# VectorE multiplies and sums two cached key pages in one operation, and eight more pages stand in the projections

## What is computed

```python
past_k = cache_k[l][page_table].reshape(n_seq, n_pages * PAGE_SIZE, B_HEADS, B_HEAD_DIM)
...
s_past = (jnp.einsum('bqhd,bkhd->bhqk', q, past_k).astype(jnp.float32) * scale
          + F_new[..., None] - F_past)
...
p = jax.nn.softmax(jnp.concatenate([s_past, s_new], axis=-1), axis=-1)
```

## Time and profile before

| | |
|---|---|
| median of 3 runs | 2400.07 us |
| lowest and highest | 2394.64, 2401.17 us |
| the profiled execution: time, span | 2381.5 us, 2379.8 us |
| TensorE busy in the span | 1949.2 us (82%) |
| VectorE busy | 1640.2 us (69%) |
| GpSimd busy | 1291.0 us (54%) |

### The profile page before, as it was taken

The page is one execution under the profiler, slowest core; times in us unless marked ns, Lnnn a source line. Parts: engine busy times, 40 slices in busy tenths (PEclk is TensorE's granted clock), DMA queues, the critical chain, the costliest instruction groups (busy, mean ns, idle before and its releaser), DMA issues.

```text
span 2379.8 us, 30517 instructions
## 1 busy us (share of the span) xinstructions
PE 1949.2 (82%) x10334; PEld 815.0 (34%) x10334; DVE 1640.2 (69%) x3898; ACT 313.1 (13%) x675; POOL 1291.0 (54%) x1562
## 2 busy tenths in 40 slices
PE   5999999897889978878886788996776766776677
PEld 4444444534556775323331133331111111111111
DVE  2898899665544388666667876577787786767642
ACT  1112233521121121110000101010000000000000
POOL 1343333144443245666667766666666666666674
PEclk8999999999999989999999999999999999999899
DMA  9786787797787569999999999999999999999997
GB/s 332 263 271 210 247 280 247 232 350 240 257 278 244 185 225 383 404 389 404 402 387 378 392 404 404 402 389 390 377 370 368 378 358 382 363 369 366 376 381 282
DMA packets 264649, 794.62 MB, mean 334 GB/s; under 512 B 33328, under 2 KB 64788, under 8 KB 263992
## 3 DMA queue, kind: packets, MB, share of 16 engines
q0 software_dynamic: 191008, 680.63, 76.9%
q1 hardware_dynamic: 73504, 112.20, 13.7%
HBM read 781.60 MB, written 11.11 MB: 333 GB/s over the span
## 4 chain that ended last, share of the span: by engine, by line
PE 28%; POOL 27%; DVE 16%; issue 13%; DMA 9%; another core or an unknown queue 6%; ACT 1%; SPq 0%; PEld 0%; POOLq 0%; DVEq 0%; PEldq 0%; ACTq 0%
POOL arena L1022 27%; PE banks L1047 11%; DVE arena L2981 5%; PE banks L1349 3%; DMA arena<-in_peer_v,arena 2%; PE banks L1480 2%; DMA arena<-in_cache_v 2%; DMA arena<-in_peer_u,arena 2%; PE banks L1684 2%; DMA arena<-in_w_ada 2%; DVE arena L2196 1%; PE banks L1225 1%; PE banks L1232 1%; DVE arena L2201 1%
## 5 line engine op out<-in xcount | busy, mean ns | idle before, releaser
L1684 PE MATMUL banks<-arena 128*32 128x512 f32 x2048 | 906.9, 625 | 302.7 <-DMA arena<-in_peer_v,arena 204.1
L2981 DVE CUSTOM_DVE_ANT_0 arena<-arena,banks 128x1024 f32<-128x1024 f32 x496 | 601.8, 1216 | 261.6 <-DMA arena<-in_peer_u,arena 187.3
L1022 POOL DMA_INDIRECT arena<-in_peer_v,arena x520 | 501.4, 964 | 305.1 <-issue 157.7
L1022 POOL DMA_INDIRECT arena<-in_peer_u,arena x520 | 504.8, 971 | 220.9 <-issue 152.6
L1684 PEld LDWEIGHTS banks<-arena 128*32 128x32 f32 x2048 | 178.1, 112 | 948.2 <-issue 528.3
L1047 PE MATMUL banks<-arena 128*128 128x128 f32 (+6 forms) x1352 | 352.0, 417 | 8.9 <-DVE arena L2259 2.7
L1753 ACT ACTIVATE arena<-banks 128x512 f32<-128x512 f32 (+12 forms) x360 | 154.5, 429 | 1163.1 <-remote 263.2
L998 POOL DMA_DIRECT2D arena<-in_cache_k x256 | 137.8, 538 | 282.5 <-DVE arena L2201 184.8
L1047 PEld LDWEIGHTS banks<-arena 128*128 128x128 f32 (+1 forms) x1352 | 216.6, 195 | 146.0 <-issue 129.2
L998 POOL DMA_DIRECT2D arena<-in_cache_v x256 | 138.4, 541 | 224.5 <-PE banks L1349 169.0
L2196 DVE TENSOR_TENSOR arena<-arena 128x512 f32<-128x512 f32 x256 | 175.0, 684 | 20.1 <-DMA arena<-scratch_queries 17.5
(11 more groups left out here) (307 smaller groups left out, 1615.8 us busy)
## 6 DMA issues: line engine op xcount, KB each, us to landing
arena<-in_cache_k POOLq DMA_DIRECT2D x256, 256.0 KB, 3.5
arena<-in_cache_v POOLq DMA_DIRECT2D x256, 256.0 KB, 4.3
arena<-in_w_ada SPq DMA_DIRECT2D x12, 2048.0 KB, 14.1
arena<-in_w_in SPq DMA_DIRECT2D x10, 2048.0 KB, 13.5
arena<-in_peer_wq SPq DMA_DIRECT2D x16, 1024.0 KB
arena<-in_peer_u,arena POOLq DMA_INDIRECT x520
arena<-in_peer_v,arena POOLq DMA_INDIRECT x520
scratch_gates<-arena SPq DMA_DIRECT2D x16, 256.0 KB, 3.7
```

The lines of the kernel that those rows point to most:

```text
L1022: nc.gpsimd.indirect_dma_start(gathered[:, j, :], None, tables[kind[0]][:, :], OFF(ap=index, axis=0)).then_inc(row_in[j], 16)
L1684: ins = mm(acc[u][32 * j:32 * (j + 1), :], spread[:, n % 2, b, :], gathered_row(("v", t, x))[:, 512 * u:512 * (u + 1)], start=x < 4, stop= ...
L2981: release(nc.vector.tensor_tensor_reduce(out=row, in0=row, in1=h2[:, t, :] if x < WIDE_AT else h2_wide, scale=1.0, scalar=0.0, op0=MUL, op ...
```

## The change

Three edits. First, `page_products(k)` multiplies pages k and k+1 in one operation of 128x1024 (the query is repeated along the pair), and `page_sums(k)` sums both; the pair is freed by one post, on the semaphore of its even slot. Of 512 page operations 256 are left, and the eight slots are used as four pairs. Second, GpSimd waits for an even slot only while it loads keys, and issues the odd one right behind. Third, `Z_PAGES` puts 2 or 4 pages ahead of a shifted block, 140 by PROJ's end instead of 132; 116 pages are left for FOX, which fill rounds 0 to 28 instead of 0 to 30.

```diff
-Z_PAGES = [96 + 2 * _m + max(0, _m - 6) for _m in range(MS + 1)]
+Z_PAGES = [96 + 2 * _m + 2 * (8 * _m // MS) for _m in range(MS + 1)]
...
-                            pool.wait_ge(page_free[j], b * 4 + g + (1 + 32 * past))
+                            if past or j % 2 == 0:
+                                pool.wait_ge(page_free[j], b * 4 + g + (1 + 32 * past if j % 2 == 0 else 1))
                             pool.dma_start(pages[:, j, :], rows_of[ds(page, 1), :, :].rearrange("o p d -> (o p) d"))\
                                 .then_inc(page_loaded[j], 16)
...
-            def page_product_of(k):
-
-                dve.wait_ge(page_loaded[k % RING], 16 * (k // RING + 1))
-                tt(pages[:, k % RING, :], pages[:, k % RING, :], qb[:, k // PAGES, :], MUL).then_inc(page_product, 1)
-
-            def page_sum_of(k):
-
-                dve.wait_ge(page_product, k + 1)
-                red(scores[:, :, k], pages[:, k % RING, :].rearrange("p (h d) -> p h d", h=H), AX.X, ADD)\
+            def page_products(k):
+
+                for j in range(k, k + 2):
+                    dve.wait_ge(page_loaded[j % RING], 16 * (j // RING + 1))
+                two = pages[:, k % RING:k % RING + 2, :]
+                tt(two, two, along(qb[:, k // PAGES, :], [P, 2, W], 1), MUL).then_inc(page_product, 1)
+
+            def page_sums(k):
+
+                dve.wait_ge(page_product, k // 2 + 1)
+                red(scores[:, :, k:k + 2].rearrange("p h j -> p j h"),
+                    pages[:, k % RING:k % RING + 2, :].rearrange("p j (h d) -> p j h d", h=H), AX.X, ADD)\
                     .then_inc(page_free[k % RING], 1)
 
             def page_dots(a, b):
 
-                for k in range(a, b):
-                    page_product_of(k)
+                for k in range(a, b, 2):
+                    page_products(k)
                     if k:
-                        page_sum_of(k - 1)
+                        page_sums(k - 2)
                 if b == NS * PAGES:
-                    page_sum_of(b - 1)
+                    page_sums(b - 2)
```

## The result

| | before | changed |
|---|---|---|
| median | 2396.91 us (6 runs) | 2416.23 us (6 runs) |
| lowest and highest | 2392.65, 2401.17 us | 2410.79, 2426.11 us |
| profiled execution: time, span | 2381.5, 2379.8 us | 2417.5, 2415.9 us |
| TensorE's first matmul of FOX starts | 255.2 us | 267.5 us |
| FOX, from there to the first matmul behind the heads | 193.3 us | 199.4 us |

The ratio is 1.0074, 95% interval 1.0056 to 1.0093: some 18 us slower. The forecast was +3.3 us and the range ended at 2411.0, so it was wrong, and wrong on the side of the second rival. The two profiled executions are 36 us apart: 12.3 us are there when FOX begins, 6.1 more when it ends (448.5 against 466.9 us), and the rest comes in the phases behind it, which the change does not touch.

What follows compares the result with a forecast made beforehand. TensorE was taken to bound PROJ, and TensorE and VectorE neck and neck FOX. FOX's gain -2.8, slot stalls +6.1 and PROJ's pages 0 sum to +3.3 us on 2400.1: 2403.4 us, range 2394 to 2411.

Steps and rivals of the forecast that it cites:

- the second rival: Late and cold: VectorE reaches the last shifted block 2 us late and TensorE's clock falls; +9.5 us, 2409.6; chance 0.18.
- part 1: Page operations: a pair costs 2.27 us instead of 2.39, saving 15.4 us of VectorE over 128 pairs.
- part 2: FOX, if pages come in time: TensorE's waits for ScalarE shrink, -2.8 us; bounds 0 and -5.2.
- part 3: Page slots: no spare time for refills, so three weight loads in FOX stall VectorE 3.0 us each; +6.1 us.
- the refill just about keeps up: In a row of pages, a refill takes 4.2 to 4.8 us against 4.5 between a sum and the slot's next product.
- part 4: PROJ: eight pages cost 9.1 us, 66 pairs save 7.9, loads 12 to 18, against 14.7 idle; taken 0, up to +3.
- The refills keep up: Weight bursts make way or fall where VectorE waits anyway, so FOX gains 2.8 us; 2397.3 us, chance 0.27.
- Late and cold: The second rival: late last shifted block, 2 us, plus 1.5 clock falls of 2.8 us in FOX; 2409.6 us, chance 0.18.
- The wide operations save nothing: Three-dimensional shapes cost VectorE its 0.12 us a pair, leaving only the slots' cost, +6.1 us, 2406.2; chance 0.05.

Runs made afterwards that it cites:

- the second profile: The changed kernel as it is, run again beside the kernel before on another occasion: 2400.92 us, ratio 1.0060.
- the three kernels named above: Kernel before with 140 pages in PROJ, 1.0004; kernel before with small weight loads, 1.0009; changed kernel with direct sums, 140 pages, first run, 0.9983.
- the slowest kernel above: Kernel before with single pages, each sum behind the product of three pages later, and 140 pages in PROJ: 2413.38 us, ratio 1.0116.

## Why the prediction was wrong, step by step

**The operations (part 1): right.** 1221 ns against 1220; a pair takes 2.26 us against 2.27; VectorE is 14.1 us less busy (1640.2 to 1626.1) against "some 14". The rule of the Trainium skill (VectorE: DVE Perf Modes, The TRN2 errata) that the fixed cost is paid between instructions would have saved 40 us; this trace does not agree, with 14.1, and it was rightly set aside: the starts of two operations in a row decide.

**What FOX gains (part 2): too large, as far as it can be measured.** Only the kernel with small loads has pairs at 2.26 us with few late pages in FOX. Its FOX takes 190.4 us, 2.9 less than before, for 2.8 forecast; but that is no proof, since FOX differs by 3.7 us between the two profiles of the same kernel with direct sums (195.8, 192.1), nearly all of it TensorE's busy time. Part 2 spoke of TensorE's waits for ScalarE, and those are 5.3 us there, against 7.1 before and 6.2 with single pages and the same small loads: a gain of 0.9 to 1.8 us.

**The slots (part 3): the mechanism right, the size too small.** Spare time of 0 to 0.3 us where there had been 3, stalls a few us after a weight load, landings of 6 to 7 us: all there. The step that failed here is "the refill just about keeps up" in a row of pages, with loads as the only disturbance. In FOX each of the three loads stopped VectorE for 3.1 to 3.8 us (1.64 + 2.15; 3.07; 1.67 + 1.80), near the 3.0 of the forecast, 10.3 us in all; 3.4 us more were lost in smaller pieces, most of them away from loads. The sum was 13.7 us (16.6 less the 2.9 that belong to PROJ) against 9. FOX became 6.1 us longer (8.8 in the second profile, 5.3 with the late sums in FOX alone) where -2.8 + 6.1 = +3.3 was forecast. How much of the page waits the waits for TensorE covered can't be read from these lengths, since the slower matmuls are in them: in the last of these three kernels 14.3 us of page waits made TensorE's waits for ScalarE 1.9 us longer, and its matmuls 3.7.

**Eight more pages in PROJ (part 4): the step that broke the forecast.** It had the right account: 14.7 us idle, 9.1 spent on pages, 7.9 won. It put the stalls at 12 to 18 us and then "took 0". (Four loads of 3 us to five of 4 us are 12 to 20 us; the 18 was an error of the sum.) The six loads cost 2.68, 2.71, 2.52, 3.54, 1.19 and 2.19 us with the first wait behind each, 14.8 us: the total was right, by six shorter stalls in place of four or five of 3 to 4 us. The other 7.1 of the 21.9 us are second pieces and waits away from loads, which the step did not have. Then came a term that the prediction did not think of at all: a VectorE that is late meets the next load, at 253 us, and loses 2.9 us more. In all 21.9 + 2.9 + 9.1 - 7.9 = 26.0 us against 14.7, 11 us too late; 10.3 were measured. Even by its own numbers the middle was 16 us against 14.7, so 0 was not the middle of that step but its low end.

**The rivals.** "The refills keep up" fell with the first profile. "Late and cold" is what happened, with its own size wrong: it priced the lateness at 2 us, and it was 9 to 10. Its other half, the clock, is in the rows and is no small part. Two times in FOX of the changed kernel a wait of TensorE for ScalarE is followed by slow matmuls:

```profile
337.65 1.12 PE L1218 MATMUL banks<-arena 128*64 128x128 f32 x8 [1.45 <-ACT arena L1754]
338.70 4.75 PE L1226 MATMUL banks<-arena 128*128 128x512 f32 x8
```

where such eight take 3.6 to 3.7 us. The other are the eight at 376.6 us, with 4.57, after a wait of 2.48. The granted clock was 0.97 from 311 to 437 us, where it was 1.00 before. These two and the shorter matmuls ahead of them make most of the 2.6 us above, of FOX's 6.1; in the second profile two such eights take 5.29 and 5.65 us, the granted clock is 0.95 in the same window, and slower matmuls are 6.8 of the 8.8. The rival's 1.5 falls of 2.8 us, 4.2, lie between the two. What makes the clock fall stays open: it did so in these kernels after waits of 1.5 to 2.5 us, but also twice in each of the three kernels named above, after waits of 1.0 to 1.2 us that the kernel before and the second profile of direct sums had as well, without a fall. No experiment was made on the clock alone. "The wide operations save nothing" is not what VectorE's rows show, where a pair of pages takes 2.26 us instead of 2.39; but with direct sums nothing of it reaches the time, and that it is worth 0.5 per cent when VectorE is late rests on the one comparison with the slowest kernel above.

**The chances.** The slots' shortage had 0.68 of the chance in the forecast and the second rival, and both were given small prices, for what was known to be a sum close to the edge: 13 to 19 us against 14.7. In such a place the cost is nothing or a microsecond for each microsecond, all the way to the end, so the middle should have held 16 - 14.7 = 1.3 us for it. The range was not too narrow for the terms that it had: the upper ends of the stalls (19 - 14.7 = 4.3 us in PROJ, 9.0 - 2.8 = 6.2 in FOX) make 10.5 us, and it allowed 11 above the 2400.1. What went beyond it had no term: the waits away from loads and in second pieces (7.1 us in PROJ, 3.4 in FOX) and the load met late (2.9).

## What to carry to other kernels

When operations are merged that also free the buffers they read, count the time from the release of a buffer to its next use before and after, and set it beside the refill: here the merge saved 14 us of an engine and cut that time from 7.2 to 4.5 us, and refills of 4 to 9 us then took back 38 in waits. Where an engine's idle time is the cover for a new cost, add up everything that draws on it (here 25 us of waits and 9 of added work against 14.7 idle and 7.9 saved), since each microsecond beyond it lands whole on the path, and a late engine meets transfers that it used to miss. To order the release directly behind its operation cured it at once, and cost just what the merge had won. And before one profile's stage length is set against another's, split it into work and waits: here the same matmuls took from 181.8 to 186.3 us in kernels without late pages in FOX.

## What the runs showed of the hardware

- A weight load of 2 MB holds up the pages issued in the first 6 us behind it, with pages in pairs as well as singly: 5.6 to 7.5 us to land in place of 3.1. The hope that a smaller queue of pages would let the burst pass more quickly is gone.
- Key pages land late by up to 2 us (5.0 in place of 3.1) also where no weight load runs. With single pages summed late by one, all page waits together were 1.1 us or less. With four pairs summed late, and the weight loads made small, such waits came to 10.3 us in PROJ and 3.3 in FOX.
- On VectorE an operation that waits for the one just ahead, whose result it reads, starts 0.12 us later than one that does not (1.25 and 1.13 us for 1024 columns). Placed directly behind its product, a sum over two pages gives back all that the merge wins.
- Of FOX's 980 matmuls, eights that take 3.6 to 3.7 us took 4.4 to 5.9 us now and then. Behind the first pair of heads it happened twice or more in every kernel with scarce slots and large loads in FOX, where the granted clock from 311 to 437 us was 0.93 to 0.97; twice in three kernels with no page wait above 0.2 us in FOX, where it was 0.99; and not at all in the others, where it was 1.00.
- The phases behind FOX, the same in all kernels, took from 1931 to 1949 us; two profiles of the same changed kernel had 1949.0 and 1933.0. In the profile of the kernel with late sums in FOX alone, the 5.4 us at the end of FOX are 16.4 at the end of the program.
